# A hybrid decoder step: another order for the first head pair and the top-k, key products in place on GpSimd, merges ahead of key sums

## The reference

```python
u, cB, cC, q, k, v, qi, ki, wi, qm, g = split_proj(x, pos, w_in, b_gate)   # one 1024 x 6216 projection
conv_out = short_conv(u, cB, cC, ...)                  # branch A
# branch B: an indexer scores keys, the best k are kept, attention runs over these
sc = einsum(relu(qi . ki), wi)
_, idx = top_k(sc, 64)            # prompt; 256 of 2049 keys for each sampled token
attn_out = softmax(q . k[idx] / 8) @ v[idx]            # 8 heads; the sampled keys and values come from the paged cache
mem_out = softmax(qm . mk / 8) @ mv                    # branch C, 4 heads, 256 memory tokens
m = g0 * (conv_out @ w_br_conv) + g1 * (attn_out @ w_br_attn) + g2 * (mem_out @ w_br_mem)
h = layernorm(alpha * x + m @ w_o)
y = layernorm(alpha * h + hier_moe(h))                 # top group, top 2 of 8 experts in it, 32 experts
```

## Time and profile before

| | |
|---|---|
| median of 3 runs | 612.38 us (610.49 to 614.92) |
| the profiled execution | 612.95 us, its span 611.1 us |
| TensorE busy | 551.1 us, 90% of the span |
| VectorE, ScalarE, GpSimd busy | 277.9, 101.1, 63.9 us |
| mean granted clock of TensorE | 0.954 of full speed |
| bytes over DMA | 163.5 MB |

### The profile page before, as it was taken

One profiled execution on the slowest core, in us unless ns is written; L12 is line 12 of the kernel. 1 busy time (PEld: TensorE's weight loads), 2 busy tenths in 40 slices (PEclk: granted clock), 3 DMA queues, 4 the chain that ended last, 5 costly groups with the idle time before them and its releaser, 6 DMA issues.

```text
span 611.1 us, 8674 instructions
## 1 busy us (share of the span) xinstructions
PE 551.1 (90%) x3518; PEld 348.4 (57%) x3518; DVE 277.9 (45%) x766; ACT 101.1 (17%) x243; POOL 63.9 (10%) x70
## 2 busy tenths in 40 slices
PE   7999999999999995999799899999999995987671
PEld 4556566475688773777576456766654661522120
DVE  1273765666677687759862496312010200100026
ACT  1001111011310123545100211011101110101011
POOL 0000000000200034587200000000000000000002
PEclk9999999998999996999899997999999999897796
DMA  8981231944443445576869926899999999999971
GB/s 294 372 321 45 93 138 50 365 140 140 131 132 120 139 138 189 175 242 190 330 247 403 321 70 262 306 417 388 424 390 422 420 419 420 422 419 421 417 302 71
DMA packets 47886, 163.53 MB, mean 268 GB/s; under 512 B 5954, under 2 KB 22812, under 8 KB 35812
## 3 DMA queue, kind: packets, MB, share of 16 engines
q1 hardware_dynamic: 39280, 139.81, 59.4%
q0 software_dynamic: 3472, 14.31, 6.9%
q10 hardware_dynamic: 5092, 8.83, 4.0%
HBM read 160.14 MB, written 2.77 MB: 267 GB/s over the span
## 4 chain that ended last, share of the span: by engine, by line
PE 57%; DMA 17%; DVE 17%; ACTq 5%; issue 2%; ACT 1%; SPq 0%; POOLq 0%; POOL 0%; DVEq 0%
PE bank L578 11%; DMA ring<-in_w_down 10%; PE bank L769 10%; PE bank L1122 6%; DMA ring<-in_w_up 5%; PE bank L539 4%; PE bank L1214 2%; PE bank L965 2%; ACTq L1476 2%; PE bank L624 2%; ACTq L1475 2%; DVE ring L1686 2%; PE bank L1079 2%; PE bank L1097 2%; PE bank L592 2%
## 5 line engine op out<-in xcount | busy, mean ns | idle before, releaser
L769 PE MATMUL bank<-work,ring 128*128 128x264 f32 x384 | 94.1, 396 | 0.0
L578 PE MATMUL bank<-ring,work 128*128 128x512 f32 (+2 forms) x224 | 90.6, 544 | 2.1 <-DMA ring<-in_w_in 2.1
L769 PEld LDWEIGHTS bank<-work,ring 128*128 128x128 f32 x384 | 71.2, 192 | 14.8 <-issue 2.8
L1122 PE MATMUL bank<-ring,work 128*32 128x512 f32 x304 | 52.4, 665 | 14.2 <-DMA ring<-in_w_up 11.0
L578 PEld LDWEIGHTS bank<-ring,work 128*128 128x128 f32 x224 | 40.0, 190 | 32.8 <-issue 29.7
L2350 DVE SCALAR_TENSOR_TENSOR work<-work,bank 128x256 f32<-128x256 f32 x8 | 3.4, 422 | 87.0 <-ACT work L1530 87.0
L2362 DVE COPY gates<-bank 128x512 f32<-128x512 f32 x8 | 5.5, 692 | 74.7 <-PE bank L1214 67.7
L895 PE MATMUL bank<-work,ring 128*128 128x264 f32 x128 | 32.6, 400 | 4.3 <-DVE gates L2091 4.3
L1122 PEld LDWEIGHTS bank<-ring,work 128*32 128x32 f32 x304 | 13.9, 121 | 37.5 <-issue 37.4
L1122 PE MATMUL bank<-proj,work 128*32 128x512 f32 x128 | 30.6, 622 | 2.3 <-DMA ring<-in_w_up 1.9
L895 PEld LDWEIGHTS bank<-work,ring 128*128 128x128 f32 x128 | 24.0, 195 | 12.5 <-DVE gates L2091 5.1
(11 more groups left out here) (337 smaller groups left out, 845.1 us busy)
## 6 DMA issues: line engine op xcount, KB each, us to landing
ring<-in_w_up SPq DMA_DIRECT2D x19, 2048.0 KB, 19.8
ring<-in_w_down SPq DMA_DIRECT2D x13, 2048.0 KB, 24.3
...
```

The source lines that it names most:

```text
L578: last = mm(bank[2 * (i % 2) + t][:, 0:w], lhs[:, k, 128 * t:128 * t + 128], rhs[:, k % 4, :], start=(k == 0), stop=(k == KT - 1))
L769: last = mm(b[:, 0:TOK], w[:, k, 128 * (n % 2):128 * (n % 2) + 128], xT[:, k, 0:TOK], start=(k == 0), stop=(k == KT - 1))
L1122: last = mm(bank[5][32 * j:32 * j + 32, :], xTe[q // 2 % 2][:, k, s0:s0 + CAP], up_of(n + j // 2, j % 2, r), start=(k == 0), stop=(k == KT ...
```

## The change

It makes seven edits.

- **Constants:** ScalarE asks for the table of constants (882 KB) when the first unit of `w_in` is there, and no longer when the prompt is.
- **First head pair:** `scores(0)` moves ahead of `gate_tile(11)` on TensorE; for memory heads VectorE takes the maximum straight from the score bank, and ScalarE's `exps` reads that bank. In each pair `scores(p + 1)` now stands between the two turns, for the first pair with half a gate tile.
- **Top-k:** all 16 rounds run in the first two pairs of the loop (3, 5, 3 and 5); before, eight ran between the indexer's steps.
- **Head output:** ScalarE stores it and not VectorE.
- **Gathers:** the 16 gathers of keys go out with no wait between them. Two gathers of values follow, and the rest stand between and behind the key products, with no wait for the head pairs.
- **Key products:** all 17 on GpSimd, in place, with no wait for VectorE's sums; VectorE sums 4, 4, 5, 3 and 1 rows in one instruction each.
- **Merges:** `merge(2)` stands ahead of the last key sums, and the others move one place or more ahead between the steps of the sampled attention; TensorE's tiles move with them.

```diff
--- before.py
+++ after.py
@@ tables of the key products and sums @@
-VALUE_GATHERS = ((), range(0, 4), range(4, 8), range(8, 12), range(12, 16), ())
-KEY_PRODUCTS = ((), range(0, 3), range(3, 6), range(6, 9), range(9, 12), ())
-KEY_SUMS = ((), (), range(0, 3), range(3, 6), range(6, 9), range(9, 12))
-KEY_DOTS = ((), (), range(12, 13), range(13, 15), range(15, 17), ())
-NPROD, NDOT = 12, 5
+KEY_SUMS = ((), (), ((0, 4),), ((4, 8),), ((8, 13),), ((13, 16), (16, 17)))
+NSUMS = sum(len(x) for x in KEY_SUMS)
...
                 if n == NU_WO:
-                    sp.wait_ge(kd_mul, NPROD)
-                    sp.wait_ge(kd_dot, NDOT)
+                    sp.wait_ge(kd_sum, NSUMS)
...
                     pe.wait_ge(is_act, len(INDEX_STEPS))
+                elif p == 2:
+                    pe.wait_ge(at_e, 4 * p)
...
             gate_tile(10)
             index_scores(0)
+            scores(0)
             gate_tile(11)
...
             index_scores(2)
-            scores(0)
             gate_tile(13, part=0)
...
             for p in range(PAIRS_H):
                 turn(2 * p)
-                turn(2 * p + 1)
                 if p + 1 < PAIRS_H:
                     scores(p + 1)
-                ahead, behind = PAIR_TILES[p]
                 if p == 0:
                     gate_tile(14, part=1)
+                turn(2 * p + 1)
+                ahead, behind = PAIR_TILES[p]
                 if ahead is not None:
                     gate_tile(ahead)
                 if p == PAIRS_H - 1:
                     branch_tile(3)
-                    sample_max(1, H)
                     branch_tile(4)
-                    branch_tile(5)
-                    sample_spread(1, H)
                 values(p)
                 if behind is not None:
                     gate_tile(behind)
                 if p == PAIRS_H - 2:
                     for j in range(3):
                         branch_tile(j)
+            branch_tile(5)
+            sample_max(1, H)
             branch_tile(6)
+            sample_spread(1, H)
             branch_tile(7)
+            branch_tile(8)
             sample_sum(1, H)
-            branch_tile(8)
             branch_tile(9)
...
             act.dma_start(ident, a["consts"][:, 0:128]).then_inc(id_in, 16)
-            act.wait_ge(x2_in, 16)
-            act.dma_start(cst[:, 128:nconst], a["consts"][:, 128:nconst]).then_inc(cst_in, 16)
...
+            act.wait_ge(unit_sem(0), UC[0])
+            act.dma_start(cst[:, 128:nconst], a["consts"][:, 128:nconst]).then_inc(cst_in, 16)
...
             def exps(n):
                 act.wait_ge(at_m, n + 1)
+                if n >= 2:
+                    act.wait_ge(at_t, n - 1)
                 st = 8 * (n % 2)
                 for t in range(2):
                     at, w = keys_of(t, n)
                     s = P1[n % 2][:, at:at + w]
-                    act.activation(s, s, ACT.Exp, bias=stats[:, st + t:st + t + 1],
+                    src, scale = (score_bank(n)[:, at:at + w], 0.125) if n < NMH else (s, 1.0)
+                    act.activation(s, src, ACT.Exp, bias=stats[:, st + t:st + t + 1], scale=scale,
                                    accum_out=stats[:, st + 2 + t:st + 3 + t]).then_inc(at_e, 1)
...
+            def head_out(p):
+                act.wait_ge(at_v, 2 * p + 2)
+                dst = memoT[:, p, 0:256] if 2 * p < NMH else attnT[:, p - NMH // 2, 0:256]
+                act.activation(dst, bank[4][:, 0:256], ACT.Copy).then_inc(at_oe, 1)
+
+            index_relu(0)
+            index_relu(1)
+            gate_out(11)
+            exps(0)
+            gate_out(12)
+            normalise(0)
             index_relu(2)
             index_relu(3)
-            exps(0)
+            exps(1)
             index_relu(4)
-            exps(1)
-            normalise(0)
+            normalise(1)
             gate_out(13)
             index_relu(5)
-            normalise(1)
...
                     normalise(2 * p + 3)
+                head_out(p)
...
-            for i in range(16):
-                if i >= 2:
-                    pool.wait_ge(kg_in[i % 2], 16 * (i // 2))
+            def key_gather(i):
                 pool.indirect_dma_start(Kg[:, i, :], None, ck,
-                                        bass.IndirectOffsetOnAxis(ap=idx_sb[:, i:i + 1], axis=0))\
-                    .then_inc(kg_in[i % 2], 16)
-            pool.wait_ge(sa_p, 4)
-
-            def key_product(i):
-                if i == 0:
-                    pool.wait_ge(kg_in[0], 16 * 8)
-                    pool.wait_ge(kg_in[1], 16 * 8)
-                    pool.wait_ge(qr_sb, 1)
-                    pool.wait_ge(is_dve, len(INDEX_STEPS))
-                if i >= 4:
-                    pool.wait_ge(kd_sum, i - 3)
-                pool.tensor_tensor(prod[i % 4], Kg[:, i, :], qrep, ALU.mult).then_inc(kd_mul, 1)
+                                        bass.IndirectOffsetOnAxis(ap=idx_sb[:, i:i + 1], axis=0)).then_inc(kg_in, 16)
 
             def value_gather(i):
                 pool.indirect_dma_start(Vg[:, i, :], None, cv,
                                         bass.IndirectOffsetOnAxis(ap=idx_sb[:, i:i + 1], axis=0)).then_inc(vg_in, 16)
 
-            for p in range(1, PAIRS_H - 1):
-                pool.wait_ge(at_t, 2 * p + 1)
-                products, gathers = list(KEY_PRODUCTS[p]), list(VALUE_GATHERS[p])
-                for i in range(4):
-                    value_gather(gathers[i])
-                    if i < len(products):
-                        key_product(products[i])
+            def key_product(i):
+                row = Kg[:, i, :] if i < 16 else knew
+                pool.tensor_tensor(row, row, qrep, ALU.mult).then_inc(kd_mul, 1)
+
+            for i in range(16):
+                key_gather(i)
+            pool.wait_ge(sa_p, 4)
+            value_gather(0)
+            value_gather(1)
+            pool.wait_ge(qr_sb, 1)
+            pool.wait_ge(knew_in, 32)
+            pool.wait_ge(kg_in, 16 * 16)
+            for i in range(17):
+                key_product(i)
+                if i % 2 == 1 and 2 + i // 2 < 9:
+                    value_gather(2 + i // 2)
+            for i in range(9, 16):
+                value_gather(i)
...
-            def key_sum(i):
-                dve.wait_ge(kd_mul, i + 1)
-                link(V.tensor_reduce(ssc[:, H * i:H * i + H], heads_of(prod[i % 4]), AX.X, ALU.add), kd_sum)
-
-            def key_dot(i):
-                if i == NPROD:
-                    dve.wait_ge(kg_in[0], 16 * 8)
-                    dve.wait_ge(kg_in[1], 16 * 8)
-                    dve.wait_ge(knew_in, 32)
-                    dve.wait_ge(qr_sb, 1)
-                row = Kg[:, i, :] if i < 16 else knew
-                tt(row, row, qrep, ALU.mult)
-                link(V.tensor_reduce(ssc[:, H * i:H * i + H], heads_of(row), AX.X, ALU.add), kd_dot)
+            def key_sum(i0, i1):
+                dve.wait_ge(kd_mul, i1)
+                n = i1 - i0
+                rows = Kg[:, i0:i1, :] if i0 < 16 else knew.unsqueeze(1)
+                link(V.tensor_reduce(ssc[:, H * i0:H * i1].rearrange("p (i h) -> p i h", i=n),
+                                     rows.rearrange("p i (h d) -> p i h d", d=HD), AX.X, ALU.add), kd_sum)
...
+                if n < NMH:
+                    link(V.tensor_reduce(st[:, 0:2], score_bank(n)[:, :].rearrange("p (t n) -> p t n", t=2),
+                                         AX.X, ALU.max, negate=True))
+                    ts(st[:, 0:2], st[:, 0:2], 0.125, s=at_m)
+                    return
...
             tt(Alo, Alo, scan[:, 0:128].unsqueeze(2).broadcast_to([128, 128, 16]), ALU.mult, comp_in)
+            softmax(0)
             dve.wait_ge(comp_ps, 4)
...
             for p in range(PAIRS_H):
-                r0, r1, r2 = TOPK_ROUNDS[p]
+                r0, r1, r2, r3 = TOPK_ROUNDS[p]
                 for i in range(r0, r1):
                     topk_round(i)
                 if p + 1 < PAIRS_H:
                     softmax(2 * p + 2)
                     softmax(2 * p + 3)
-                sums = list(KEY_SUMS[p])
-                for part in (0, 1):
-                    for i in sums[part:part + 1]:
-                        key_sum(i)
-                    if p + 1 < PAIRS_H:
-                        inverse(2 * p + 2 + part)
-                for i in sums[2:]:
-                    key_sum(i)
-                if p + 1 < PAIRS_H:
                     for i in range(r1, r2):
                         topk_round(i)
-                    head_out(p)
-                    for i in KEY_DOTS[p]:
-                        key_dot(i)
+                    inverse(2 * p + 2)
+                    if p == PAIRS_H - 2:
+                        for i0, i1 in KEY_SUMS[p]:
+                            key_sum(i0, i1)
+                    inverse(2 * p + 3)
+                    for i in range(r2, r3):
+                        topk_round(i)
+                    if p < PAIRS_H - 2:
+                        for i0, i1 in KEY_SUMS[p]:
```

(20 more changed lines are left out.)

83 lines of the change are left out of this document (32 added, 51 removed).

## The result

The changed kernel takes **618.84 us** (median of 4 runs, 616.17 to 619.56) where the kernel before takes 611.43 beside it (4 runs, 609.91 to 614.92): ratio 1.0106, 95% interval 1.006 to 1.0153. It is slower by 1%, and the forecast was 598. The profiled execution took 616.17 us, its span 614.4.

The account below looks back on a forecast made before the run. Routing on TensorE was taken to hold back the memory-bound expert stream, so savings before `sample_values` carry through. Terms -9.8 - 0.4 - 5.9 + 0.3 + 1.7 - 1.0 = -15.1 from 612.95 gave 597.9, stated as 598; range 594 to 604.

Parts of the forecast that it names:

- Term: 0: GpSimd's list of gathers and products: dropping the pauses between gathers costs TensorE nothing, with 9 us of slack.
- GpSimd becomes the bound: Rival: products waiting for VectorE and slow gathers end GpSimd's list at 317, giving 624 us; chance 0.04.
- First head pair: TensorE's waits and low clock around the first two turns go: -9.8 us, and -0.4 for a wait at the row numbers.
- top-k: The mask, wanted before `softmax(4)`, is ready just in time: counted 0, or 2 us at the range's other end.
- the mask's slack of 0.7 us: The third pair's softmaxes, behind the mask, finish near 253 us, and TensorE wants the last at 253.5.
- Branch tiles and sampled attention: Wait for the first merge and low clock behind it go, -5.9 and +0.3; later waits add +1.7 us.
- The wait ahead of `sample_values`: TensorE waits 1.9 us for VectorE before `sample_values`, where it waited 0.78 us.
- Products against VectorE: GpSimd's products shut out only VectorE operations with two SBUF inputs; the mask's last addition remains, 0 to 0.6 us on TensorE.
- Slack of 9 us: GpSimd's list ends at 283 us, while `sample_values` wants the gathered values at 294.
- I give the landing 1 us: Time allowed for gathered rows to land, given where key gathers end at 240 and two value gathers at 242.4 us.
- Constants: At the start, asking later for constants lets the first unit land sooner and TensorE's first chunk start earlier: -1.0 us.
- Behind `sample_values`: The stretch from `sample_values` to the end stays about as long, 299 us, so earlier savings carry to the end.

Follow-up runs that it names:

- e4: The kernel before with only the wait ahead of each key gather taken out; 623.01 us, ratio 1.0171.
- e16: e13 with one small VectorE operation put back, the one behind the maximum of head 1; 618.35 us, ratio 1.0085.
- e17: e13 with two small VectorE operations put back, those of heads 2 and 3; 618.03 us, ratio 1.0092.
- e13: The changed kernel with the memory heads' factor 0.125 put on ScalarE's query copies instead of four small VectorE operations; 596.78 us, ratio 0.9736.
- e9: e13 with another GpSimd list: six paused key gathers, then key gathers alternating with products, then two value gathers per product; 597.41 us, ratio 0.9755.
- e8: The changed kernel with key gathers of half the bytes (wrong half rows), the other half filled with zeros beforehand; 600.25 us in one run.
- e7: The kernel before with the new order of first pair, top-k, turns and scores, head outputs on ScalarE and late constants; 608.52 us, ratio 0.9944.
- e12: The kernel before with merges, branch tiles and sampled steps in the new order and head outputs on ScalarE; 613.22 us, ratio 1.0004.
- e10: e9 without the scaled query copies, so with the four small VectorE operations back; 605.82 us, ratio 0.9892.
- e3: The changed kernel with a fill of zeros between key gathers on GpSimd and no wait for a landing; 608.99 us, ratio 0.9947.
- e11: The changed kernel with at most three key gathers under way, three semaphores in turn; 603.37 us, ratio 0.9839.
- e1: The changed kernel with the old pauses back: key gathers wait for the landing two places ahead; 612.85 us, ratio 1.0.

## Why the prediction was wrong

**The step that failed** is the sentence "Nobody waits for the pauses between gathers today; what counts is when the list ends", and its "Term: 0". Nobody waits for the pauses, but they keep something from going wrong: without them, the increments of TensorE's semaphores came up to 15 us late. Without pauses the middle is 9.4 us longer in the kernel before (97.38 in `e4`) and 18 to 19 in the changed one where it stalls (92.17 and 93.30 in `e16` and `e17`, against 74.13 in `e13`, which has no pauses either and does not). None of my rivals had it, and the median of 618.84 lies above 618.5, the bound for slower, which had a chance of 0.04. "GpSimd becomes the bound" had the right sign for another reason: products took 1.25 us, the last ended at 272.98 (forecast 275) and the list at 282 (283).

**The other terms.** In `e13` nothing stalls, and its middle is 87.98 - 74.13 = 13.85 us shorter. The forecast without the constants was -9.8 - 0.4 - 5.9 + 0.3 + 1.7 = -14.1. So first pair, top-k, branch tiles and list are right as a sum:
- *First head pair* and *top-k*: in `e13`, `e9` and `e8` TensorE is busy 10.00 of 10 us from 220 to 250, and the mask's slack of 0.7 us ends as a wait of 0.97, 0.20 and 1.01 at `turn(4)`. Alone (`e7`) they shorten the middle by 6.5, not 10.2: what was saved is partly waited for later.
- *Branch tiles and sampled attention*: forecast -3.9, alone -1.7 (`e12`). All parts together give 13.85 where these two alone give 6.5 + 1.7. The rest needs both parts or the new list on GpSimd, which neither `e7` nor `e12` has; no run tells which. The forecast added the terms as if apart and was right only for all of them. The wait ahead of `sample_values`, forecast 1.9, is 1.74 in nearly every version.
- *Products against VectorE*: wrong as put, "two inputs from SBUF". TENSOR_SCALAR with one input and two columns waits for products as well. The same section of the Trainium skill that I drew on, page "SBUF — State Buffer", "Who interferes with whom", says so: `tensor_scalar`, `copy` and `cast` can run in a mode with both ports and then lock GpSimd out or are locked out. I took its two-input rule and left that one; by that rule, the traces agree (0.17 against 1.21, 2.91, 1.78 and 1.68 us). The same section of the Trainium skill holds that a DMA never contends with a compute engine. In this case TensorE's increments come late while gathers are under way, with no VectorE operation that explains it, and no run shows whether a port takes part. In the changed kernel the loss lies behind the larger one: with the stall, `e16` lacks the operations of heads 2 and 3 and takes 618.35, `e17` has them and takes 618.03. Without it they cost 6.3 in the middle of `e10`, where products start at 231.8; in the changed kernel they start at 243.7, and what they would cost there without a stall wasn't tried.
- *Slack of 9 us*: too large. "I give the landing 1 us" was for the keys, and it was 243.69 - 238.42 = 5.3 from the end of the last key gather's issue. Of values the last needs 7.7 us from the end of its issue behind seven close ones (`e3`, `e11`). A list that ends at 284 just does.
- *Constants*, forecast -1.0: the first chunk starts 0.12 earlier; over all twenty profiles it starts between 10.18 and 10.38 with the constants late (fourteen), and between 10.15 and 10.54 with them early (six). The term was put too high by nearly all of it.
- *Behind `sample_values`*: as said, the saving is carried: behind its start 303.3 us before and 303.0 in `e13`. In `e16` and `e17` it is 307.9 and 307.7, so there the stalled kernels lose again behind it, which was not followed up.

**Was 598 right for a reason?** `e9` and `e13` took 597.4 and 596.8. Both lack what the forecast had left out: the small operations by their edit, and the stall in `e13` by luck of the batch and in `e9` by pace or by the same luck. So the forecast was right about the order of work and wrong about what runs beside it.

**What stays open.** Why TensorE's increments are held. Pace matters: in the first batch `e4` stalled and `e1` and `e3` did not. Whether bytes do is not shown. A high load of the DMA engines is not enough: from 222 to 228 us the gathers' packets take 68.8% of the DMA engines' time in `e13`, without a stall, and 69.4% in `e17`, with one (28.8% in `e8`). In order, window 222 to 228 of `e13` and of `e17` (queue, packets, MB, share):

```profile
q0 software_dynamic: 356, 1.20, 68.8%
```
```profile
q0 software_dynamic: 373, 1.23, 69.4%
```

What differs between these two is the batch: the chip, where something lies in memory, or a state of the chip that comes and goes; no run tells them apart. Nor was one made without recording, which could itself take part, since records are missing where increments are late. Nor has a way past the stall but pace been tried in a batch that stalls: `e13` has the lowest median, but in such a batch it may well take 618. `e9`, with a key gather every 2.4 us, is the version I would keep, for the pace that helped in `e1` and `e3`. It ran in one batch at 597.4 us, and with early constants in another at 599.0, and neither batch had a stall. That it holds in one that has is not shown, and its value gathers leave in pairs 1.3 us apart.
